# Taps of the depthwise convolution shared by ScalarE and VectorE, and half of a projection's weights split ahead of time through memory

## The reference

```python
def conformer_conv(h, pw1, pw1_b, dw, dw_b, ln_g, ln_b, pw2, pw2_b):
    z = h @ pw1 + pw1_b                       # 2048 -> 4096
    z = z[..., :D] * sigmoid(z[..., D:])      # the gate
    z = causal_dwconv(z, dw) + dw_b           # 31 taps per channel, over tokens
    z = silu(layernorm(z, ln_g, ln_b))        # over the 2048 channels
    return z @ pw2 + pw2_b
```

## Time and profile before

| what | value |
|---|---|
| median of 3 runs | 2246.91 us (2244.43 to 2247.08) |
| the profiled execution: time | 2245.52 us |
| the profiled execution: span | 2243.7 us, mean granted TensorE clock 0.992 |
| busy: PE / DVE / ACT / POOL | 97% / 69% / 43% / 0% of the span |
| start of MLP0, of PW1, of PW2 on PE | 521.5, 1193.7, 1462.3 us |
| HBM read | 393.49 MB, 176 GB/s over the span |

### The profile page before, as it was taken

How to read it: one execution, slowest core, us unless ns; L and a number is a source line. 1 busy time by engine, 2 the same in 40 slices (tenths; PEclk the granted TensorE clock), 3 DMA queues, 4 the chain that set the end, 5 groups by cost and what they waited for, 6 DMA issues and landing times.

```text
span 2243.7 us, 35720 instructions
## 1 busy us (share of the span) xinstructions
PE 2167.5 (97%) x13992; PEld 2007.4 (89%) x13992; DVE 1551.7 (69%) x1802; ACT 969.7 (43%) x1039; POOL 8.8 (0%) x20
## 2 busy tenths in 40 slices
PE   7998998999999999999999999899999999999998
PEld 7988898899999999999998888788899999999997
DVE  7767657667756756756774999977665665665666
ACT  4544344444544544544541100264444444444454
POOL 0000000000000000000000000000000000000000
PEclk9999999999999999999999999999999999999999
DMA  5434234355555555555554444244555555555554
GB/s 220 177 119 138 96 112 132 122 201 197 205 205 206 190 203 206 194 199 206 199 194 150 150 150 150 94 139 180 188 207 194 199 206 198 195 206 203 190 206 150
DMA packets 56445, 396.94 MB, mean 177 GB/s; under 512 B 6560, under 2 KB 6944, under 8 KB 9248
## 3 DMA queue, kind: packets, MB, share of 16 engines
q1 hardware_dynamic: 55008, 391.42, 48.5%
q0 software_dynamic: 768, 2.10, 0.5%
q10 hardware_dynamic: 576, 2.10, 0.3%
HBM read 393.49 MB, written 2.10 MB: 176 GB/s over the span
## 4 chain that ended last, share of the span: by engine, by line
PE 77%; DVE 14%; issue 4%; ACT 3%; DMA 1%; DVEq 0%; ACTq 0%; SPq 0%
PE ps L1057 40%; PE ps L1059 20%; DVE work L936 4%; PE ps L1109 4%; DVE wlo L595 4%; PE ps L1032 3%; PE ps L1036 3%; PE ps L1034 3%; PE ps L1168 3%; ACT whi L274 1%; DMA raw<-in_wts 1%; DVE sq_part L635 1%; DVE work L702 0%; PE ps L1075 0%; PE ps L1163 0%
## 5 line engine op out<-in xcount | busy, mean ns | idle before, releaser
L595 DVE TENSOR_TENSOR wlo<-raw,whi 128x1024 fp32r<-128x1024 f32 x672 | 817.0, 1223 | 490.3 <-ACT whi L274 476.8
L274 ACT ACTIVATE whi<-raw 128x1024 fp32r<-128x1024 f32 x672 | 705.7, 1057 | 709.1 <-PE ps L1059 369.1
L1057 PE MATMUL ps<-hid,whi 128*128 128x512 f32 x2240 | 734.9, 382 | 5.7 <-DVE hid L969 3.3
L1057 PE MATMUL ps<-xg,whi 128*128 128x512 f32 x2048 | 674.8, 383 | 6.7 <-ACT sq_part L319 4.3
L1059 PE MATMUL ps<-hid,wlo 128*128 128x256 f32 x2240 | 610.6, 273 | 0.0
L1059 PE MATMUL ps<-xg,wlo 128*128 128x256 f32 x2048 | 559.6, 273 | 0.0
L1057 PEld LDWEIGHTS ps<-hid,whi 128*128 128x128 f32 x2240 | 423.3, 189 | 66.3 <-issue 3.9
L1057 PEld LDWEIGHTS ps<-xg,whi 128*128 128x128 f32 x2048 | 388.5, 190 | 62.3 <-ACT sq_part L319 4.9
L1059 PEld LDWEIGHTS ps<-hid,wlo 128*128 128x128 f32 x2240 | 430.1, 192 | 0.0
L1059 PEld LDWEIGHTS ps<-xg,wlo 128*128 128x128 f32 x2048 | 394.5, 193 | 0.0
L1032 PE MATMUL ps<-xg,whi 128*128 128x256 f32 x768 | 220.4, 287 | 12.6 <-DVE wlo L595 12.6
(11 more groups left out here) (212 smaller groups left out, 1475.6 us busy)
## 6 DMA issues: line engine op xcount, KB each, us to landing
raw<-in_wts SPq DMA_DIRECT2D x368, 1024.0 KB, 4.8
x<-in_xt SPq DMA_DIRECT2D x4, 512.0 KB, 8.5
x<-in_xt ACTq DMA_DIRECT2D x4, 512.0 KB, 3.7
work<-in_rows POOLq DMA_DIRECT2D x12, 128.0 KB, 4.0
out_t<-work SPq DMA_DIRECT2D x3, 512.0 KB, 2.7
ct<-in_consts SPq DMA_DIRECT2D x1, 768.0 KB, 6.3
work<-in_w_s POOLq DMA_DIRECT2D x4, 128.0 KB, 4.4
out_t<-work SPq DMA_DIRECT2D x2, 256.0 KB, 2.9
```

Of the source, the lines that this page charges most:

```text
L274: nc.scalar.activation(whi[:, i % SPLIT].rearrange("p a b -> p (a b)"), raw[:, r, HALF * (i % 2):HALF * (i % 2) + HALF], ACT.Copy).then_in ...
L595: tt(wlo[:, i % SPLIT].rearrange("p a b -> p (a b)"), raw[:, i // 2 % RAW, HALF * (i % 2):HALF * (i % 2) + HALF], whi[:, i % SPLIT].rearra ...
L1057: mm(ps[:, 4 * par + n, :], whi[:, r, k, cols], woven_parts(operand[:, kt]), start=(kt == 0), stop=False)
```

## The change

1. **PW1's first 8 of 16 input tiles are multiplied as split products.** Their weights (16 MB of the 32 MB, new input `pw1`) are split during MLP0: in each of the 32 groups `pre_high_part` (ScalarE) and `pre_low_part` (VectorE) handle one half chunk of 128x1024, between the sixth and seventh half of the group's own weights. ScalarE's queue issues the load of the next half (`pre_load`) and the stores of the last one's two parts (`pre_store`) to two memory tensors `pw_hi` and `pw_lo`. In PW1, SP loads both back into `whi` and `wlo` (`pw_load`), and the other eight input tiles still as `raw` (`pw_chunk`).
2. **PW1 is 16 groups of one value tile and one gate tile** (`pw1_group`): 16 products of three fp32r MATMULs and 16 of two float32 passes. For input tiles 0 to 7 `norm_part` now makes the split operand `xg`, two more copies on ScalarE and two more subtractions on VectorE near the end of MLP0.
3. **Taps.** ScalarE makes 24 of 31 products of a tile (`tap_products`, each into its own 128x256 slot of `prods`, a ring of four blocks of eight). VectorE adds the three blocks (128x2048), folds eight to one (1024, 512, 256), and runs the other 7 taps itself; `add_folds` joins both. Of group g VectorE does the adding during group g+1.
4. **LayerNorm sums.** POOL adds the pivot to the first 8 tiles and accumulates sum and sum of squares of tiles 0 to 14; ScalarE squares tile by tile; TensorE multiplies only the two accumulators and the last tile with ones. After the four high parts for PW2, ScalarE computes one root of a single column ahead of the last two squares.

```diff
-            def convolve(i, par, first):
...
-                for k in range(WD):
-                    for t in range(2):
...
-                            ins = stt(acc[t], src, w, acc[t], ALU.mult, ALU.add)
+            for g in range(KT):
+                par = 2 * (g % 2)
+                dve.wait_ge(pw_used, 3 * g + 3)
+                tt(halves(total[:, par:par + 2, :]), in_order(ps[:, par:par + 2, 0:T]), halves(by_token(rms[:], 2)),
+                   ALU.mult).then_inc(s["glu_scaled"], 1)
+                if g:
+                    add_blocks(g - 1, 1)
+                gated(g)
+                tap(g, 0)
+                if g:
+                    add_blocks(g - 1, 2)
+                tap(g, 1)
+                if g:
+                    fold(g - 1, 4)
...
+            def tap_products(g):
+                act.wait_ge(s["z_new"], g + 1)
+                for b in range(BLOCKS):
+                    n = BLOCKS * g + b
+                    if n >= RING:
+                        before, part = divmod(n - RING, BLOCKS)
+                        act.wait_ge(s["blocks"], (BLOCKS - 1) * before + max(part, 1))
+                    for i in range(BLOCK_TAPS):
+                        k = BLOCK_TAPS * b + i
+                        dst, w = prods[:, n % RING, i, :], dwt[:, g, k:k + 1]
+                        if k:
+                            ins = nc.scalar.activation(dst, window(g, k), ACT.Copy, scale=w)
...
+            def pre_high_part(q, j):
+                p, n = j % 2, 8 * q + j
+                act.wait_ge(pre_low, n + 1)
+                if not isinstance(q, int) or n:
+                    act.wait_ge(pre_high, n)
+                    pre_store(n - 1, 1 - p)
+                if not isinstance(q, int) or n < PRE - 1:
+                    pre_load(n + 1, 1 - p)
+                act.wait_ge(pre_in[p], 16 * (4 * q + j // 2 + 1))
+                act.wait_ge(pre_hi_out[p], 16 * (4 * q + j // 2 + 1))
+                copy(pre_hi[p][:], pre_raw[p][:]).then_inc(pre_high, 1)
...
+            def pre_low_part(q, j):
+                p, n = j % 2, 8 * q + j
+                dve.wait_ge(pre_high, n + 1)
+                dve.wait_ge(pre_lo_out[p], 16 * (4 * q + j // 2 + 1))
+                tt(pre_lo[p][:], pre_raw[p][:], pre_hi[p][:].bitcast(F32), ALU.subtract).then_inc(pre_low, 1)
...
+            def pw1_group(g):
+                par = 2 * (g % 2)
...
+                            mm(dst, hi[:, cols], woven(xg[:, kt, 0, :]), start=(kt == 0), stop=False)
+                            mm(dst, hi[:, cols], woven(xg[:, kt, 1, :]), start=False, stop=False)
+                            ins = mm(dst, lo[:, cols], woven(xg[:, kt, 0, :]), start=False, stop=False)
...
+            pe.wait_ge(s["sq_used"], KT - 1)
+            pe.wait_ge(s["ln_sums"], KT + 1)
+            mm(ps[:, 0, 0:T], const("ones"), ln_sum, start=True, stop=False)
+            mm(ps[:, 1, 0:T], const("ones"), ln_sum_sq, start=True, stop=False)
...
+            for t in range(KT - 1):
...
+                nc.gpsimd.tensor_tensor(ln_sum, ln_sum, conv[:, t, :], ALU.add).then_inc(s["ln_sums"], 1)
+                pool.wait_ge(s["ln_sq"], t + 1)
...
+                nc.gpsimd.tensor_tensor(ln_sum_sq, ln_sum_sq, ln_squares[:, t % 2, :], ALU.add).then_inc(s["sq_used"], 1)
```

Behind the first normalization of the LayerNorm VectorE now has two of the four low parts that stood ahead of the statistics:

```diff
-            for i in range(4):
-                low_part(G_PW2, i, UNSPLIT)
+            low_part(G_PW2, 0, UNSPLIT)
+            low_part(G_PW2, 1, UNSPLIT)
...
             normalize(0)
+            low_part(G_PW2, 2, UNSPLIT)
+            low_part(G_PW2, 3, UNSPLIT)
```

More of the change, by code:

```diff
@@ L133, in build @@
         hi_ready, lo_ready = sem("hi_ready"), sem("lo_ready")
-        raw_used = sem("raw_used")
+        pw_used = sem("pw_used")
+        pre_in = [sem(f"pre_in{p}") for p in range(2)]
+        pre_hi_out, pre_lo_out = ([sem(f"pre_{n}_out{p}") for p in range(2)] for n in ("hi", "lo"))
+        pre_high, pre_low = sem("pre_high"), sem("pre_low")
+        pw_hi_in, pw_lo_in = ([sem(f"pw_{n}_in{r}") for r in range(SPLIT)] for n in ("hi", "lo"))
         half_free = sem("half_free")
@@ L216, in _ @@
             sp.dma_start(pt[:], params).then_inc(const_in, 16)
+            sp.sem_inc(pre_low, 1)
+            for p in range(2):
+                sp.sem_inc(pre_hi_out[p], 16)
+                sp.sem_inc(pre_lo_out[p], 16)
             for j in range(4):
@@ L524, in _, with window, gate @@
-            ins.then_inc(s["acc_init"], 1)
-            with act.Fori(1, 4) as i:
-                for par in range(2):
-                    gate(i, par)
-            act.wait_ge(raw_used, 4 * UNSPLIT)
-            act.wait_ge(s["first_ln_d"], 1)
-            squares(1, slice(0, 4))
-            squares(3, slice(4, 8))
-            squares(5, slice(8, 12))
+            def window(g, k):
+                return zwin[:, g % 4, 2 + k:2 + k + T]
+            def gate(g):
+                act.wait_ge(s["glu_scaled"], g + 1)
+                w = total[:, 2 * (g % 2) + 1, :]
+                nc.scalar.activation(w, w, ACT.Sigmoid, bias=gate_bias[:, g:g + 1]).then_inc(s["gate"], 1)
@@ L939, in _, with block_of @@
[L939 to L950 removed]
+            def block_of(g, b):
+                return prods[:, (BLOCKS * g + b) % RING]
@@ new lines, in gated @@
+            def gated(g):
+                dve.wait_ge(s["gate"], g + 1)
+                par = 2 * (g % 2)
+                stt(zwin[:, g % 4, 32:32 + T], total[:, par, :], param("pw1_b")[:, g:g + 1], total[:, par + 1, :],
+                    ALU.add, ALU.mult).then_inc(s["z_new"], 1)
+                dve.wait_ge(s["z_new"], g + 1)
+            for g in range(KT):
+                par = 2 * (g % 2)
[11 more added lines that the diff above has]
+                    fold(g - 1, 4)
+                tap(g, 2)
+                if g:
+                    fold(g - 1, 2)
+                tap(g, 3)
+                if g:
+                    fold(g - 1, 1)
+                tap(g, 4)
+                if g:
+                    add_folds(g - 1)
+                tap(g, 5)
+                tap(g, 6)
@@ L1329, in _, with idle_products @@
-            ins.then_inc(s["ln_stats"], 1)
+            for g in range(KT):
+                pw1_group(g)
+            def idle_products(n):
+                for _ in range(n):
+                    mm(ps[:, 4, 0:T], const("ones"), conv[:, 0, :], start=True, stop=True)
+            pe.wait_ge(banks_free, G_PW1 + 2)
+            pe.wait_ge(s["pivoted"], 1)
+            for i in range(DVE_TAPS):
+                pe.wait_ge(s["taps"], DVE_TAPS * (KT - 1) + i + 1)
+                idle_products(2)
+            pe.wait_ge(s["z_new"], KT - 1)
```

336 lines of the change are left out of this document (209 added, 127 removed).

## The result

The changed kernel takes **2261.95 us** (median of 5 runs, 2255.52 to 2264.18); the kernel before took 2246.29 beside it (5 runs, 2244.07 to 2247.08). The ratio is 1.0064, 95% interval [1.0051, 1.0076]: slower by about 15 us, where 23 us faster was forecast.

The account below looks back on a forecast made before the run. TensorE was taken to bound MLP0 and PW1, with a 46.3 us VectorE tail behind PW1. Terms -24 + 6 - 7 + 2 = -23 from 2245.5 gave 2222.5, as a median 2223 us; forecast range 2215 to 2231 (chance 0.50).

Parts of the forecast that it names:

- TensorE in PW1: PW1's products on TensorE: 16 groups of 48 fp32r MATMULs and 32 float32 passes take 198.4 us, minus 24 us.
- MLP0 at +2 us: MLP0: 32 groups cost 0; split operands in groups 29 and 30 add 2 us, bounds 0 and 6.
- Engines' work at no cost: MLP0: the added splitting on ScalarE and VectorE fits their spare time, cost 0 for the 32 groups.
- a lead of 5.5: MLP0: halves split ahead of TensorE leave 5.5 us of cover for late parts and chunks.
- first pair is issued 7.8 us before MLP0's end: Seam from MLP0 to PW1: PW1's first pair of split weights goes out 7.8 us before MLP0 ends.
- Rival C: MLP0: splitting ahead breaks the rhythm, TensorE waits 2.2 us in every group, 70 us, 2293 us; chance 0.10.
- GpSimd: PW1's last ten groups: 38 GpSimd additions may hold VectorE up, plus 6 us, bounds 0 and 19.
- the 13 us of room that the forecast counted: PW1's last ten groups: VectorE's spare time, 1.3 us a group, that absorbs 13 us of GpSimd's hindrance.
- Rival A: PW1: GpSimd holds VectorE up in full, 0.85 us an addition, 19 us of lag, 2236 us; chance 0.15.
- B: PW1: ScalarE becomes the bound, products at 0.49 us each, 19 us in place of GpSimd's lag, 2236; chance 0.12.
- The tail: PW1's end on TensorE to PW2: 39 us instead of 46.3, minus 7 us, bounds minus 10 and minus 2.
- -24 - 1 + 2 = -23: Whole kernel: PW1 on TensorE -24, GpSimd's lag +6 with the tail -7, MLP0 +2, 23 us faster.

Follow-up runs that it names:

- e1: The changed kernel with xf stored in woven memory order, so its float32 passes read it contiguously: 2231.81 us, ratio to before 0.9935.
- e2: The kernel before, with its 1024 float32 passes of PW1 reading xf in woven order: 2300.15 us, ratio 1.0241.
- e4: The changed kernel splitting only the first two half chunks ahead in MLP0, moving nothing more (wrong weights in half of PW1): 2249.63 us, ratio 1.0016.
- e5: The changed kernel splitting in all 32 groups of MLP0, but loading and storing only the first two parts (wrong weights): 2248.52 us, ratio 1.0011.
- e9: On e1 with a reordered tail: each group's 1.5 MB of split-ahead transfers given out at three places, not together: 2245.13 us, ratio to before 0.9979.
- e6: e1 without 30 of GpSimd's additions for the LayerNorm sums (statistics incomplete): 2231.59 us, ratio to before 0.9930.
- e12: e1 with a reordered tail, nothing split ahead, and all of PW1 in float32 from raw; shared taps kept: 2236.67 us, ratio to before 0.9954.
- e3: The changed kernel with all of PW1 in token order, fp32r products and float32 passes reading contiguously: 2235.85 us, ratio to before 0.9953.

## Why the prediction was wrong

**The failed step** is in the forecast's "TensorE in PW1": "A float32 pass takes 60/280 = 0.2143 us", applied to 512 passes that now read their operand woven. The last sentence of the text names it as something "which no row shows and I take as equal". It had no bounds in the sum and no rival of its own, although the diff put `woven(...)` around an operand that the kernel before read plain. It measured 0.273 us: 512 x 0.059 = 30 us, the difference between 198.4 and 228.9; e1 and e2 show that the pattern is the cause. The sum itself said how much hung on it: 23 us over 512 passes are 0.045 us a pass, a fifth of its price, and the whole gain is gone. An unknown of that weight needs a bound, a chance or a measurement of its own.

**The second miss is a size**: MLP0 at +2 us with an upper bound of 6, measured +13.4 (e1: +12.7). Engines' work at no cost was right (e4, e5). The bursts were taken to delay one chunk of four by 3 us, inside a lead of 5.5. In fact ScalarE's waits for chunks went from 96 to 250 us and used the lead up, so that the last groups and the seam, where operands, stores and PW1's first loads come together, had none. The forecast's "first pair is issued 7.8 us before MLP0's end" leaves out the two `raw` chunks ahead of it in SP's program: it was 4.8 us (4.0 in e5), and from the issue to TensorE's first product it took 10 us (6.9 in e5). Rival C had this mechanism, with a price of 2.2 us for every group; it was 2.5 us for the 31 groups up to 1170 us, 0.08 each, and 11 us at the end. The place was wrong, and the seam as a place of its own was missing. What makes the transfers cost as much as they do, beyond their bytes, stays open (e9).

**GpSimd**: +6 us forecast, none in the changed kernel, where the slower passes gave VectorE 3 us of room a group (the failed step hid this term); 2.5 in e1. The forecast took half of what 0.63 us an addition would leave; it is 0.43 (e1 and e6), so that 38 additions make 16 us, 3 more than the 13 us of room that the forecast counted. Rival A (0.85) is out, and so is B: ScalarE's 23 products take 9.29 us in the tail of after, 0.40 each.

**The tail** was right: 38.9 for 39, with its intermediate times. TensorE's granted clock was 0.50 from 1457 to 1460 us, after an idle stretch, and the 20 products took 6.5 us where the forecast had 6.8. In e1 the tail was 41.6, the same with the lag of 2.5 added.

With the operand in order, e1's profile gives -21.8 (PW1) - 4.7 (tail and lag) + 12.7 (MLP0) = -13.8, where the forecast had -24 - 1 + 2 = -23, and e1 measured 14 us less than before. Once the pass has its price PW1 is 2.2 us short of its term and the tail with its lag 3.7 us better; MLP0's 10.7 us are what keeps e1 9 us short of the forecast. (2223 was itself 0.9 us low: 2222.5 and 1.4 are 2223.9.)

## What to carry to other kernels

A product's price belongs to its type, its size and the way it reads its moving operand, together: when a diff changes the access pattern of an operand in the bound engine's inner loop, price that as an edit of its own, and keep for each precision the order that it reads fastest. Work moved ahead into a stage that streams weights was paid here in transfers, not in engine time: look at who waits for the stream, how much lead it leaves, and spend that lead's end, the seam to the next stage, as a term of its own. Where a change has two parts with one mechanism each, a kernel with only one of them (e12) says what each is worth.

## What the runs showed of the hardware

- A float32 pass over 256 columns takes 0.214 us with a contiguous moving operand and 0.273 with the woven one (neighbours 512 bytes apart); an fp32r product takes 0.1176 and 0.1117: the two types prefer opposite orders (e1, e2, e3). Other distances were not tried.
- VectorE and GpSimd hold each other up, and GpSimd loses more by it. From e1's group at 1385 us:

```profile
1387.22 0.91 POOL L324 TENSOR_TENSOR rest<-rest,work 128x256 f32<-128x256 f32 x1
1388.09 0.91 POOL L328 TENSOR_TENSOR rest<-rest 128x256 f32<-128x256 f32 x1
1388.95 2.78 POOL L324 TENSOR_TENSOR rest<-rest,work 128x256 f32<-128x256 f32 x1
```
```profile
1384.39 2.28 DVE L1061 TENSOR_TENSOR rest<-prods 128x2048 f32<-128x2048 f32 x1
...
1388.33 2.81 DVE L1061 TENSOR_TENSOR rest<-rest,prods 128x2048 f32<-128x2048 f32 x1
1391.07 0.95 DVE L1084 SCALAR_TENSOR_TENSOR work<-work,dwt 128x256 f32<-128x256 f32 x1
...
1393.07 0.47 DVE L1084 SCALAR_TENSOR_TENSOR work<-work,dwt 128x256 f32<-128x256 f32 x1
```

  A GpSimd addition of 128x256 takes 0.72 us alone (the tail above) and up to 2.8 beside a long VectorE instruction; a VectorE instruction that meets one is longer by about 0.5 us, whether it lasts 0.47 or 2.28. The Trainium skill (SBUF — State Buffer, on the shared ports) has the two exclude each other for a whole instruction. These rows agree: VectorE's addition that starts at 1388.33 is 0.53 us longer, where GpSimd's of 1388.09 has 0.67 us left, and GpSimd's of 1388.95 ends 0.6 us after VectorE's of 1388.33. So each waits for what is left of the other's instruction; the 0.43 us that an addition cost VectorE on average (e6) is less than the 0.72 of a whole one. GpSimd's spans are rough, so this is a reading that fits and not a proof. An estimate for the addition from the skill's measured 2048 elements (GPSIMD Engine Reference, section 3.1), scaled to 256, is 0.56 us; 0.72 was measured.
